# Modulation groups moved from TensorE to VectorE, and three norms whose root is applied after the matmuls

## What is computed

```python
def rmsnorm(x, g):
    y = xf * lax.rsqrt(jnp.mean(xf * xf, axis=-1, keepdims=True) + RMS_EPS)
    return y * g
h = h + swiglu(rmsnorm(h, norm_ffn_g[layer]), w1, w3, w2)   # (silu(hn@w1) * (hn@w3)) @ w2, both layers
kv_a = rmsnorm(h, norm_kv_g) @ w_kv_a                       # MLA, then rmsnorm of kv_a's 512 columns
cq   = rmsnorm(rmsnorm(h, norm_mix_g[1]) @ w_q_a, q_a_norm_g)
mod  = silu(c) @ w_mod + b_mod                              # 1024 -> 6144, one row for all tokens
sh1, sc1, g1, sh2, sc2, g2 = split(mod)                     # shift, scale, gate: used in the second part only
h = rms_norm(x, norm1_w) * (1.0 + sc1) + sh1
```

## Time and profile before

| | us |
|---|---|
| median of 3 runs | 1372.31 (1371.7 to 1374.33) |
| span of the profiled execution | 1368.2 |
| PE busy / VectorE busy / ScalarE busy | 1324.9 / 760.7 / 601.4 |
| feed-forward 0 and `down0` | about 259 to 459 |
| `kva` to the end of MLA's heads | 466 to 605 |
| `wo1`, feed-forward 1, `down1` | 605 to 826 |
| experts | from about 1110 |

### The profile page before, as it was taken

How to read it: one execution, slowest core, us unless ns; L and a number is a source line. 1 busy time by engine, 2 the same in 40 slices (tenths; PEclk the granted TensorE clock), 3 DMA queues, 4 the chain that set the end, 5 groups by cost and what they waited for, 6 DMA issues and landing times.

```text
span 1368.2 us, 25178 instructions
## 1 busy us (share of the span) xinstructions
PE 1324.9 (97%) x9648; PEld 1140.5 (83%) x9648; DVE 760.7 (56%) x1378; ACT 601.4 (44%) x1012; POOL 27.0 (2%) x44
## 2 busy tenths in 40 slices
PE   6999999999999999999999999999999999999887
PEld 5999999899999898768999998998999974444344
DVE  6466656656655677446666556868745752222214
ACT  5545554533434565445444446566644441111112
POOL 0000020000000000000000000000000000000100
PEclk9999999999999999999999999999999999999999
DMA  9774355754555654277555556442223499999992
GB/s 367 167 234 154 125 177 167 258 179 173 170 180 175 249 162 141 80 294 256 188 186 185 186 185 239 162 139 78 62 93 117 164 359 383 416 418 418 419 419 108
DMA packets 83142, 295.27 MB, mean 216 GB/s; under 512 B 11046, under 2 KB 12070, under 8 KB 82912
## 3 DMA queue, kind: packets, MB, share of 16 engines
q1 hardware_dynamic: 78480, 284.65, 57.3%
q0 software_dynamic: 4560, 9.16, 2.9%
HBM read 287.24 MB, written 11.53 MB: 218 GB/s over the span
## 4 chain that ended last, share of the span: by engine, by line
PE 89%; DVE 4%; ACT 2%; DMA 2%; issue 1%; SPq 1%; DVEq 0%; ACTq 0%
PE bank L812 19%; PE bank L816 19%; PE bank L815 19%; PE bank L1504 11%; PE bank L1015 2%; DMA w_late<-weights 1%; PE bank L1459 1%; PE bank L940 1%; PE bank L898 1%; ACT w_hi L1600 1%; PE bank L1460 1%; DVE ring_low L2066 1%; PE bank L955 1%; PE bank L1305 1%; PE bank L836 1%
## 5 line engine op out<-in xcount | busy, mean ns | idle before, releaser
L2066 DVE TENSOR_TENSOR ring_low<-ring,w_hi 128x1024 fp32r<-128x1024 f32 x292 | 356.0, 1224 | 234.3 <-ACT w_hi L1600 231.7
L812 PE MATMUL bank<-hn_hi,w_hi 128*128 128x272 f32 (+1 forms) x1416 | 410.3, 290 | 4.6 <-DVE hn_low L2087 3.9
L816 PE MATMUL bank<-hn_hi,ring_low 128*128 128x272 f32 (+1 forms) x1416 | 404.5, 286 | 0.0
L815 PE MATMUL bank<-hn_low,w_hi 128*128 128x272 f32 (+1 forms) x1416 | 403.6, 285 | 0.0
L1600 ACT ACTIVATE w_hi<-ring 128x1024 fp32r<-128x1024 f32 x292 | 306.3, 1054 | 193.0 <-PE bank L812 169.1
L812 PEld LDWEIGHTS bank<-hn_hi,w_hi 128*128 128x128 f32 x1416 | 267.5, 189 | 8.8 <-DVE hn_low L2087 5.1
L816 PEld LDWEIGHTS bank<-hn_hi,ring_low 128*128 128x128 f32 x1416 | 267.7, 189 | 0.0
L815 PEld LDWEIGHTS bank<-hn_low,w_hi 128*128 128x128 f32 x1416 | 267.3, 189 | 0.2
L812 PE MATMUL bank<-arena_r,w_hi 128*128 128x256 f32 (+1 forms) x816 | 233.6, 286 | 2.9 <-DVE arena L2268 2.2
L816 PE MATMUL bank<-arena_r,ring_low 128*128 128x256 f32 (+1 forms) x816 | 232.1, 284 | 0.0
L815 PE MATMUL bank<-arena_r,w_hi 128*128 128x272 f32 (+1 forms) x752 | 213.8, 284 | 0.0
(11 more groups left out here) (441 smaller groups left out, 1607.5 us busy)
## 6 DMA issues: line engine op xcount, KB each, us to landing
ring<-weights SPq DMA_DIRECT2D x436, 512.0 KB, 3.5
tab<-weights SPq DMA_DIRECT2D x32, 512.0 KB, 12.6
arena<-weights SPq DMA_DIRECT2D x29, 512.0 KB, 13.2
w_late<-weights SPq DMA_DIRECT2D x28, 512.0 KB, 12.8
tab<-tables SPq DMA_DIRECT2D x1, 2858.0 KB, 17.3
skew<-arena POOLq DMA_DIRECT2D x1, 2048.0 KB, 48.3
expert_rows<-mod_part POOLq DMA_DIRECT2D x4, 512.0 KB, 31.8
h<-tokens SPq DMA_DIRECT2D x2, 544.0 KB, 4.4
```

The source lines that it names most:

```text
L812: begun = mm(dst[:, 0:cols], wh, high(k), start=k == 0, stop=False)
L815: mm(dst[:, 0:cols], wh, low(k), start=False, stop=False)
L816: last = mm(dst[:, 0:cols], wl, high(k), start=False, stop=k == K - 1)
L2066: tt_(ring_lo[:, slot, :], ring[:, slot, :], w_hi[:, n % SPLITS, :], ALU.subtract).then_inc(S("w_lo_ready"), 1)
```

## The change

1. Groups 0 to 9 of the modulation leave PE, the ring, `mod_store` and `mod_add`. Their 5120 columns of `w_mod` come as 40 turned tiles of 128x1024 in a new tensor `mod_rows`: output feature on the partition, input on the free axis. GpSimd loads them one after the other into one buffer (`mod_row`, the memory of `mod_part`), each after VectorE has used the one before. VectorE's `mod_tile` multiplies such a tile by silu(c), spread over all partitions (`c_row`), and sums over the free axis with the bias as start value. Calls: 1 in `wo0`, 11 in each feed-forward (every second pair), 7 in `down0`, 3 in the `qa` loop, 7 in `down1`. Groups 10 and 11 stay on PE.
2. The norms `ffn0`, `mix1` with `kv`, and `ffn1` are no longer applied before the matmuls. The raw `h` times gain is split tile by tile while `wo` or `down` still runs (`high_and_square` on ScalarE, `add_and_split` on VectorE). The row sum moves behind the first two tiles. In feed-forward VectorE multiplies the w1 tile by `rstd` when it leaves PSUM, ScalarE does Silu on that in SBUF, VectorE multiplies by the w3 tile and once more by `rstd`, ScalarE copies the high part.
3. After MLA's `kva` and `qa` tiles nothing is multiplied by `rstd`, since the norms `ckv` and `cq` that follow cancel it. Only their eps must be scaled: PE adds eps times the row sum to the banks of these two norms (four more matmuls). The rotary part of `kva` is multiplied by `rstd` in `rotate`.
4. `o_m_lo` and the `kv` inputs lie elsewhere in the arena, and some semaphores are merged.

```diff
+            pool.dma_start(c_row, c_rows).then_inc(rel_loaded, 16)
+            pool.dma_start(mod_row, mod_rows[0:P, :]).then_inc(mod_loaded, 16)
...
+            for n in range(1, MOD_TILES):
+                pool.wait_ge(mod_used, n)
+                pool.dma_start(mod_row, mod_rows[n * P:(n + 1) * P, :]).then_inc(mod_loaded, 16)
...
             def feed_forward(layer, cut, cols):
-                if layer == 0:
-                    pe.wait_ge(S("c_silu"), 1)
-                mod_two(8 * layer, lambda: row_norm(f"ffn{layer}", cols))
                 dense_two(n_hi, n_lo, cols, split_ready(f"ffn{layer}"))
+                row_norm(f"ffn{layer}", cols)
...
-            mod_two(2, lambda: row_norm("mix1", T0))
             dense_two(kv_hi, kv_lo, T0, split_ready("kv"))
+            for dst, cut in ((bank[6][:, 0:T0], ALL), (bank[5][:, 0:SEQ], XC)):
+                mm(dst, eps_all, sq[:, DT - 1, cut], start=True, stop=False, skip_group_check=True)
+                mm(dst, eps_all, sq[:, 0, cut], start=False, stop=False, skip_group_check=True)
+            row_norm("mix1", T0)
...
-                if 5 <= j:
-                    mod_join(j - 1)
-                if 4 <= j < MH:
-                    mod_sum(j)
...
+            def high_and_square(first, hi, src, gain, cols):
+                for k in range(DT):
+                    highs(first + k)
+                    wait_stored(act, first + k)
+                    fn(hi(k), src(k), ACT.Copy, scale=V(gain, k)).then_inc(S("x_hi_ready"), 1)
+                    fn(sq[:, k, 0:cols], src(k), ACT.Square).then_inc(squared, 1)
...
                 for pair in range(FT):
+                    highs(first + 2 * pair)
+                    if pair:
+                        ff_high(pair - 1)
+                    wait_stored(act, first + 2 * pair)
+                    x = ff_gate[:, pair % 2, 0:cols]
+                    fn(x, x, ACT.Silu).then_inc(S("ff_silu"), 1)
...
+            def mod_tile():
+                n = mods_made[0]
+                mods_made[0] += 1
+                dve.wait_ge(mod_loaded, 16 * (n + 1))
+                nc.vector.tensor_tensor_reduce(mod_row, mod_row, c_row, 1.0, V("b_mod", n), ALU.mult, ALU.add,
+                                               mod[:, n:n + 1]).then_inc(mod_used, 1)
...
+                for k in range(DT):
+                    src, free = take(first + k)
+                    tt_(x(k), x(k), src[:, 0:cols], ALU.add).then_inc(free, 1)
+                    if k:
+                        low(k - 1)
+                    if k > 1:
+                        add_squares(name, k - 1, cols)
+                    if k in mods:
+                        mod_tile()
...
                 for pair in range(FT):
+                    tt_(x, src[:, 0:cols], r, ALU.mult).then_inc(free, 1)
+                    if pair:
+                        ff_low(pair - 1)
+                    src, free = take(t + 1)
                     tt_(x, x, src[:, 0:cols], ALU.mult).then_inc(free, 1)
+                    tt_(x, x, r, ALU.mult).then_inc(S("ff_scaled"), 1)
+                    if pair % 2:
+                        mod_tile()
...
             for t in range(3, QT):
                 lows(at["qa"] + t)
+                mod_tile()
```

More of the change, by code:

```diff
@@ L637, in build @@
         mod_summed, mod_joined = {}, {}
[L638 to L644, removed]
+        for g in range(LATE_MOD, MOD_GROUPS):
+            mod_summed[g] = at[f"mod{g // 2 * 2}"] + g % 2
+            mod_joined[g] = mod_summed[g] + 2
         norm_k = [("mix0", DT), ("ffn0", DT), ("mix1", DT), ("ckv", KVT), ("cq", QT), ("ffn1", DT), ("n1", DT),
@@ L1626, in mod_store, with root, norm @@
                 fn(mod_part[:, g % 2, :], bank[t % BANKS][:, :], ACT.Copy).then_inc(evacuated[t % BANKS], 1)
-            def norm(name, src, K, cols, width, ready, between=None, eps=RMS_EPS, total=bank[7]):
+            def root(name, cols, width, total=bank[7], bias=None):
+                act.wait_ge(summed, norm_no[name] + 1)
+                if invert_no[name]:
+                    act.wait_ge(inverted, invert_no[name])
+                fn(rms[:, 0:cols], total[:, 0:cols], ACT.Sqrt, bias=eps_col(RMS_EPS) if bias is None else bias,
+                   scale=1.0 / width).then_inc(rooted, 1)
+            def norm(name, src, K, cols, width, ready, between=None, total=bank[7]):
                 for k in range(K):
@@ L1633, in norm, with latent_norm @@
                     between()
-                act.wait_ge(summed, norm_no[name] + 1)
-                if norm_no[name]:
-                    act.wait_ge(normed, norm_out[norm_k[norm_no[name] - 1][0]] + 1)
-                fn(rms[:, 0:cols], total[:, 0:cols], ACT.Sqrt, bias=eps_col(eps), scale=1.0 / width).then_inc(rooted, 1)
+                root(name, cols, width, total)
+            def latent_norm(name, src, K, cols, ready, between, total):
+                for k in range(K):
+                    ready(k)
+                    fn(sq[:, k, 0:cols], src(k), ACT.Square, scale=math.sqrt(DT / K)).then_inc(squared, 1)
+                between()
+                root(name, cols, D, total, eps_t[:, 3:4])
+            def high_and_square(first, hi, src, gain, cols):
[4 more added lines that the diff above has]
+                    fn(sq[:, k, 0:cols], src(k), ACT.Square).then_inc(squared, 1)
             def eps_col(eps):
@@ L1819, in _ @@
             mod_store(11)
-            for g in range(2):
-                wait_stored(act, mod_joined[g])
             def shift(part, k):
@@ L2225, in add_squares, with add_and_split, low @@
                     add_square(hn, k, 1, cols)
-            add_tiles(at["wo0"], T0, lambda k: h[:, k, :], "ffn0")
+            def add_and_split(first, cols, x, name, gain, hi, lo, split, mods=()):
+                def low(k):
+                    dve.wait_ge(S("x_hi_ready"), split_first[split] + k + 1)
+                    stt(lo(k), x(k), V(gain, k), hi(k), ALU.mult, ALU.subtract).then_inc(S("x_split"), 1)
+                for k in range(DT):
[7 more added lines that the diff above has]
+                        mod_tile()
+                low(DT - 1)
```

218 lines of the change are left out of this document (117 added, 101 removed).

## The result

The changed kernel takes 1348.16 us (median of four runs, 1345.39 to 1348.99) beside 1372.63 us of the kernel before (four runs, 1371.7 to 1374.33). The ratio is 0.9816, 95% interval 0.9801 to 0.9831: 1.8% faster, 24.5 us. The prediction was 1350.6 us in a range of 1342 to 1360. The profiled execution spans 1346.8 us, 21.4 less than that of before; the prediction's sum had 21.7.

A forecast was written before the change was run, and what follows sets the result against it. TensorE (PE), busy 1324.9 of 1368.2 us, was taken to bound the kernel. Gains of 30.4 less 0.8 (VectorE) and 7.9 (`qa` stage) give 21.7 us: 1346.5 in the profile, 1350.6 as median, range 1342 to 1360.

The forecast's parts named there:

- The entries: Before `ffn0`, `kva`, `ffn1` and in MLA's loop: PE saves 6.15, 5.6, 8.0 and 10.7 us, 30.4 together.
- VectorE's load: 40 multiply-sums of 1.35 us; feed-forward's VectorE circle 5.6 us a pair, so it just keeps up: 0.8 us lost.
- the second rival: Multiply-sum dear, 2.1 us: feed-forward in layer 1 loses 8 us, about 1359 (1366 at 2.44); chance 0.12.
- The `qa` stage: Three multiply-sums close together wait for single-buffer loads; PE waits 6.3 us, plus 1.6 of clock: loss 7.9 us.
- L: Time of one 512 KB modulation tile load from GpSimd's queue, taken as 5.4 us (rows give 3.5 to 10.7).
- the slack of 2.4 us: In the `qa` stage, at the q tile: the split of `cq` could end 2.4 us later without delaying PE.
- PE's wait is 2L - 4.5: In the `qa` stage, PE idles two load times L less 4.5 us: 6.3 us at L = 5.4.
- a clock fall of 1.6 us: In the `qa` stage, PE idle that long was expected to make its clock fall once: 1.6 us more.
- rival 1: GpSimd's loads are quick, 3.2 to 3.8 us: PE waits 2 to 3 us, clock stays up, 1344.5; chance 0.16.
- 4.1 below the median, taken as constant: Whole kernel: the profiled span lies 4.1 us below the run median, so 1346.5 in the profile means 1350.6.
- the third: Single buffer starves the down projections (load of 9 us): 38 us lost against 30.4 gained, about 1380; chance 0.06.
- fourth rival: At `ffn0`, `kva` and `ffn1`, new first matmuls wait as long as the removed work took: no change; chance 0.03.

The follow-up runs named there:

- b1: The kernel before with only modulation groups 0 to 9 moved to VectorE as multiply-sums, norms left as before: 1366.91 us, ratio 0.9951.
- a3: The changed kernel without the 40 multiply-sums and 39 of their 40 loads, the bias alone in their place: 1342.18 us, ratio 0.9768.
- d1: The changed kernel with each multiply-sum done twice: 1372.02 us, ratio 1.0001 to the kernel before.
- c1: The changed kernel with two multiply-sums in the `qa` stage in place of three, the third moved to `wo0`: 1343.21 us, ratio 0.9789.
- a1: The changed kernel with the three multiply-sums of the `qa` stage moved to `wo0`: 1340.37 us, ratio 0.9764 to the kernel before.
- d2: The changed kernel with each modulation tile loaded twice, one load after the other: 1418.82 us, ratio 1.0331 to the kernel before.
- b2: The changed kernel with all modulation groups back on TensorE at their old places and no multiply-sums, only the norms changed: 1369.7 us, ratio 0.9989.

## Why the prediction was right, point by point

**The entries.** `ffn0` 6.75 (predicted 6.15), `kva` 6.37 (5.6), `ffn1` 8.53 (8.0), MLA's loop 11.02 (10.7): 32.7 us for 30.4. Each mechanism was as described. The row sum was mis-sized: at its old place it cost 1.12 us, at its new one 0.7 (why was not tested), and with the eps sums at `kva` 2.49 us where 3.36 were put down. `wo1` lost 0.4 us where 1 was assumed, and of the 11.36 us of MLA's loop 0.3 were taken back where 0.7 was assumed. The working looked at what stands between the last and the first matmul and not at busy time alone, and b1 shows why that was needed: 29 us of removed PE time are worth 7 by themselves (13 without the `qa` stage's loss).

**VectorE's load.** A multiply-sum of 1.28 us for 1.35, a circle of 5.52 us in layer 1 for the 5.6 of the sum, and 0.13 + 0.74 = 0.9 us lost for the 0.8 put down. The number was right, but it is not the multiply-sums': a3, which has none, lost 0.12 + 0.70 us at the same two places. But PE's pair in layer 1 takes 5.68 us (the distance of VectorE's multiplies L2242 in the trace before), so the margin is 0.16 us a pair. d1, with a circle made 0.6 us a pair longer, lost 10.0 us there: the second rival's arithmetic was right, its price for the sum not.

**The `qa` stage** came out near the forecast and was wrong in its parts: 6.2 us lost, 7.9 predicted. L was 4.6 and not 5.4, so the predicted wait would be 2 x 4.6 - 4.5 = 4.7. The step that failed is the slack of 2.4 us in "PE's wait is 2L - 4.5". It was taken at the q tile; but the binding place is one wait further on, where PE already stood 1.71 us before (at 523.04), and there the slack is 0.74. With it, the delay of the reciprocal, 2L - 2.16 (the formula gives 7.0, the trace 6.76), less 0.74 makes 6.0 to 6.3. By luck a third error made up for it: a clock fall of 1.6 us was added. The clock did fall (0.83 in the mean of 510 to 520 us), but while PE waited for VectorE anyway: 12.74 us from reciprocal to PE with the fall, 12.75 in c1 without.

The Trainium skill, "DMA: Bandwidth & Descriptors", section "Anatomy of one DMA", gave an estimate of 3.2 us for this load. Here the median is 4.7 us on the profile's page and the shortest 3.7, so at half DMA load the measurement decides against the Trainium skill's fit, and with it against rival 1.

**What the sum did not hold.** The profile's 21.4 us contain -0.8 us at the start and -3.4 in the second part, where nothing was changed. They are stretches at half clock, which come and go from one execution to the next. So it is luck that the profile's 21.4 us agree with the 21.7 of the sum: the places that the sum names gave 32.7 - 0.9 - 6.2 = 25.6 us, and 4.2 went where it named nothing. The changed kernel's trace has a stretch here that a1 does not have (of the experiments only c1 has one at these matmuls, and c1 lacks the one near 900 us that the others except d2 have):

```profile
1000.00:1004.00 4.00, 4.00 (x19) 4.00 (x20) 2.27 (x5) 1.06 (x1) 0.00 (x0) 0.50 0.38 131
```

and the same matmuls in a1:

```profile
993.00:996.00 3.00, 3.00 (x25) 2.87 (x26) 2.28 (x5) 1.09 (x2) 0.00 (x0) 1.00 0.46 169
```

From 840 to 1098 us (of before) seven of the experiments (all but d2) lose 1.5 us each against the trace of before, the change 3.6: the trace of before was lucky by 1.5. This is also why the step from profile to median failed. "4.1 below the median, taken as constant" was some 2.0 us that lie around the span in every run (1.85 for the changed kernel) and 2.1 of luck. With 2.0 in place of 4.1 for the changed kernel the forecast would have been 1348.5.

**Rivals.** The loads were not quick, the sum was not dear, and the third and fourth rival did not come true. d2 shows the third one alive with L doubled, and its price too low: 38 us had been worked out for L = 9, and d2 lost 71 on top of the changed kernel's 6, with some 9.5, since feed-forward 1 and the clock falls in the other stages were missing in it. What makes single loads last 7 to 8 us was not tested, so nothing here bears on the warning that the prediction cites beside this rival.

## What to carry to other kernels

Work that leaves the bounding engine gains only what the next operation was ready for: look for the chain that the removed work covered, and make both edits: here one alone gave 0.5%, the other 0.1%, both 1.8%. Where you take a slack from a trace, follow the queue to the next wait of the bounding engine and beyond: the smallest distance counts, not the nearest. A single buffer between a load and its user is fine where turns are far apart; put its turns under long tiles (here `wo0`), not three in a row ahead of a chain (6 us), and leave room for a load of nearly twice the median.

## What the runs showed of the hardware

- Loads of 512 KB that GpSimd issues took longer than SyncE's of the same size: median 4.7 us (3.7 to 7.9, 40 loads) beside 3.5 in the changed kernel, 4.7 beside 4.2 in d2. What makes the long ones was not tested.
- Behind waits of PE of 4.2 and 4.7 us the granted clock was 0.50 (b1 at 259, d2 at 440), for 18 and 15 matmuls. Before, the same fall came behind 7 us of sums of 32 columns, a row sum and joins of one column, without a long wait; but in b2 this work stands at the same three entries, and the clock fell at one only, another one. In the second part, too, such falls stand in one execution and not in another of the same instructions, 1.5 to 2 us each. So the 1.6 us of clock that the prediction took for `kva` are what the trace before shows, not a fixed price.
- A multiply-sum over 128x1024 float32 with two inputs and its result written in place takes 1.28 us, plus 0.08 for the sum; a subtraction of this size 1.22.
